# Down projection of a hybrid encoder step: two direct halves replaced by seven block products in two passes

## What is computed

```python
h = rmsnorm(x, norm_ffn_g)
gt, ffn_buf_new = causal_dwconv(h @ w_gate, ffn_buf, ffn_conv_w)
x = x + (jax.nn.silu(gt) * (h @ w_up)) @ w_down      # (640, 2816) @ (2816, 1024)
```

## Time and profile before

| | us |
|---|---|
| median of 3 runs | 945.5 (945.16 to 945.92) |
| span of the profiled execution | 943.7 |
| TensorE busy (matmuls) | 931.8, 99% |
| VectorE busy | 648.3, 69% |
| ScalarE busy | 452.1, 48% |
| GpSimd busy | 170.0, 18% |
| down projection, first to last matmul | 790.6 to 940.4 |

### The profile page before, as it was taken

One profiled execution on the slowest core, in us unless ns is written; L12 is line 12 of the kernel. 1 busy time (PEld: TensorE's weight loads), 2 busy tenths in 40 slices (PEclk: granted clock), 3 DMA queues, 4 the chain that ended last, 5 costly groups with the idle time before them and its releaser, 6 DMA issues.

```text
span 943.7 us, 16891 instructions
## 1 busy us (share of the span) xinstructions
PE 931.8 (99%) x6919; PEld 841.9 (89%) x6919; DVE 648.3 (69%) x1083; ACT 452.1 (48%) x836; POOL 170.0 (18%) x198
## 2 busy tenths in 40 slices
PE   9999999999999999999999999999999999999998
PEld 7899888998889877799888999999999999888886
DVE  7627888777775565552666999999999999435321
ACT  6634454648566454554654445444444445333310
POOL 0071101103664331000002032222222220000000
...
DMA packets 73820, 103.70 MB, mean 110 GB/s; under 512 B 2576, under 2 KB 53904, under 8 KB 73360
## 3 DMA queue, kind: packets, MB, share of 16 engines
...
## 4 chain that ended last, share of the span: by engine, by line
PE 51%; DVE 3%; ACT 2%; POOL 1%; issue 1%; ACTq 0%; POOLq 0%; DVEq 0%
PE bank L1222 8%; PE bank L1220 8%; PE bank L1221 8%; PE bank L538 5%; PE bank L537 5%; PE bank L536 5%; PE bank L484 2%; PE bank L486 1%; PE bank L485 1%; PE bank L466 1%; PE bank L562 1%; PE bank L1034 1%; PE bank L564 1%; PE bank L563 1%; PE bank L1036 1%
## 5 line engine op out<-in xcount | busy, mean ns | idle before, releaser
L2168 DVE TENSOR_TENSOR wlo<-wraw,whi 128x2048 fp32r<-128x2048 f32 (+1 forms) x56 | 126.2, 2253 | 102.2 <-ACT whi L1617 93.0
L1617 ACT ACTIVATE whi<-wraw 128x2048 fp32r<-128x2048 f32 (+1 forms) x58 | 109.3, 1885 | 101.9 <-PE bank L538 72.8
L498 PE MATMUL bank<-hhi,whi 128*128 128x320 f32 x352 | 116.4, 331 | 0.6 <-issue 0.6
L500 PE MATMUL bank<-hhi,wlo 128*128 128x320 f32 x352 | 108.7, 309 | 0.0
L499 PE MATMUL bank<-hlo,whi 128*128 128x320 f32 x352 | 108.7, 309 | 0.0
L498 PEld LDWEIGHTS bank<-hhi,whi 128*128 128x128 f32 x352 | 66.2, 188 | 5.0 <-issue 3.6
L499 PEld LDWEIGHTS bank<-hlo,whi 128*128 128x128 f32 x352 | 66.2, 188 | 3.0 <-issue 2.4
L500 PEld LDWEIGHTS bank<-hhi,wlo 128*128 128x128 f32 x352 | 66.1, 188 | 0.0
L536 PE MATMUL bank<-whi,hhi 128*128 128x512 f32 x150 | 58.4, 389 | 0.0
L537 PE MATMUL bank<-wlo,hhi 128*128 128x512 f32 x150 | 58.4, 389 | 0.0
L538 PE MATMUL bank<-whi,hlo 128*128 128x512 f32 x150 | 58.3, 389 | 0.0
...
## 6 DMA issues: line engine op xcount, KB each, us to landing
wraw<-in_w_in SPq DMA_DIRECT2D x13, 1024.0 KB, 5.5
wraw<-in_w_gate SPq DMA_DIRECT2D x11, 1024.0 KB, 5.2
wraw<-in_w_up SPq DMA_DIRECT2D x11, 1024.0 KB, 5.1
wraw<-in_w_down SPq DMA_DIRECT2D x10, 1024.0 KB, 5.1
...
wraw<-in_w_mix_out SPq DMA_DIRECT2D x4, 1024.0 KB, 6.3
...
```

Source lines behind the costliest of these rows:

```text
L498: T.matmul(o, wh[:, k, cs], hhi[:, k, hs], start=(k == 0), stop=False)
L500: ins = T.matmul(o, wl[:, k, cs], hhi[:, k, hs], start=False, stop=(k == KD - 1))
L1617: V(wv(whi, i), wv(wraw, i), ACT.Copy).then_inc(s["w_hi_ready"], 1)
L2168: V.tensor_tensor(wv(wlo, i), wv(wraw, i), wv(whi, i).bitcast(F32), ALU.subtract)\
```

## The change

The prompt's 512 rows, the 2816 numbers of the hidden width and the 1024 output columns are each split in halves. Four products of halves by halves become seven products with sums of quarters, over 11 steps each (HF = 11), since tile i of the left half goes with tile i + 11 of the right half. One product is two tiles of rows by 512 columns, six matmuls a step. The 128 sample rows are multiplied directly (`samples`, 12 matmuls a step). A weight block `B_DN[d]` now holds two row tiles (i and i + 11) over all 1024 columns, and the blocks are loaded twice: d = 0 to 10 for the first pass (products p1, p3, p5 and the samples, names `cs`), d = 11 to 21 for the second (p6, p7, p4, p2). The last two steps of the second pass are taken product by product, so that the banks end one after the other.

GpSimd makes the sums: in the first pass four of 256 numbers per partition over the activations (`first_sums`) and one of 512 over the weights (`t1_sum`); in the second pass three of 512 in place over the weight block (`block_sums`). A third sum of the activations is DVE's, within `parts_lo`. Raw blocks have four buffers now (`dn_raw`), so have their high parts (`dn_hi`). The ring of banks is fully used: the eight results p1, cs, p3, p5 (two each) take all eight, and p6, p7, p4, p2 take the same ones again. Bank by bank, ACT reads out p1 and DVE cs, p3 and p5 in round d = 13 (HF + 2), after their cuts of block 13. DVE adds the sums to the rows in rounds 14 to 17 (`more_rows`) and the rest at the end (`last_rows`).

In the diff `B_DN` is the list of the weight blocks, `s[...]` the semaphores; memory offsets, the body of `last_rows` and parts of loops that leave are cut out.

```diff
+        HF = FT // 2
+        dn_raw_at = [R2 + BLK * 4 * n for n in range(3)] + [EARLY]
+        dn_hi_at = [R2 + BLK * 4 * 3, RF, R2 + BLK * 4 * 4, R1 + 4 * BLK * 4]
...
+        def part_slot(m):
+            return 0 if m == 0 else 1 + (m - 1) % 5
+        def t1_slot(d):
+            return 0 if d == 0 else 2 - d % 2
...
+        def part_free(eng, m):
+            if m == 0:
+                passed(eng, gu_block("gate", FT // 2 - 1))
+            elif m == 1:
+                filled(eng, (("up", FT // 2 - 1), "p5"))
+            elif m < 6:
+                passed(eng, gu_block("up", FT // 2 - 1))
+            else:
+                passed(eng, B_DN[m - 5])
...
-        B_DN = [[rows(A["w_down"], k, min(4, FT - k), 512 * h) for k in range(0, FT, 4)] for h in range(2)]
...
+            blocks.append((A["w_down"].rearrange("(a f p) c -> f p a c", a=2, p=P)[n % HF], 2, D_MODEL))
+            B_DN.append(len(blocks) - 1)
...
-            down("dn", 0, B_DN[0], left_a, NT, ready_a)
-            down("dn", 1, B_DN[1], left_a, NT, ready_a)
+            def product(name, i, stationary, moving, ts=(0, 1), first=0, last=HF - 1):
+                for t in ts:
+                    c = slice(stationary[2] + t * P, stationary[2] + t * P + P)
+                    hi, lo = stationary[0][:, c], stationary[1][:, c]
+                    if i == first:
+                        take((name, t))
+                    o = bank[use[name, t][0]][:, :]
+                    T.matmul(o, hi, moving[0], start=(i == first), stop=False)
+                    T.matmul(o, hi, moving[1], start=False, stop=False)
+                    ins = T.matmul(o, lo, moving[0], start=False, stop=(i == last))
...
+            def samples(i):
...
+                    for a in range(2):
+                        ss = slice(768 + a * P, 768 + a * P + P)
+                        wh, wl = dn_weights(i, a, c)
+                        T.matmul(o, hi[:, ss], wh, start=(i == 0 and a == 0), stop=False)
+                        T.matmul(o, hi[:, ss], wl, start=False, stop=False)
+                        ins = T.matmul(o, lo[:, ss], wh, start=False, stop=(i == HF - 1 and a == 1))
...
+            for i in range(HF):
+                pe.wait_ge(s["parts_lo"], i + 1)
+                lo_cut(pe, B_DN[i])
+                product("p1", i, dn_parts(i, 0), dn_weights(i, 0, 0))
+                samples(i)
+                product("p3", i, dn_parts(i, 512), dn_weights(i, 1, 1))
+                pe.wait_ge(s["t1_lo"], i + 1)
+                ins = product("p5", i, dn_parts(i, 256), (t1_hi[t1_slot(i)][:, :], t1_lo[t1_slot(i)][:, :]))
...
+            SECOND = (("p6", 0, 0, 0), ("p7", 256, 0, 1), ("p4", 768, 1, 1), ("p2", 512, 1, 0))
+            for i in range(HF - 2):
+                d = HF + i
+                pe.wait_ge(s["parts_lo"], d + 1)
+                lo_cut(pe, B_DN[d])
...
+                step(ins, B_DN[d])
+            for name, p0, a, c in SECOND:
+                for t in range(2):
+                    for i in (HF - 2, HF - 1):
+                        d = HF + i
+                        if name == "p6" and t == 0:
+                            pe.wait_ge(s["parts_lo"], d + 1)
+                            lo_cut(pe, B_DN[d])
+                        product(name, i, dn_parts(d, p0), dn_weights(d, a, c), ts=(t,))
...
+                d = i - B_DN[0]
+                if d >= 0:
+                    if d == 3:
+                        filled(sp, (("up", FT // 2 - 1), "p5"))
+                    else:
+                        passed(sp, i - 3 if d < 3 else i - 4)
+                    D(wv(wraw, i), blocks[i][0]).then_inc(dn_loaded[d % 4], 16)
+                    return
...
+            for d in range(2, 2 * HF):
+                if d == 4:
+                    passed(sp, B_DN[0])
+                    passed(sp, gu_block("up", FT // 2 - 1))
                     sp.wait_ge(s["rows_kept"], 16)
                     D(xres[:, :, :], kept).then_inc(s["rows_back"], 16)
...
+                load_w(B_DN[d])
...
+            def first_sums(i):
+                raw, left, right = part_raw[part_slot(i)], act[:, i, 0:512], act[:, HF + i, 0:512]
+                part_free(pool, i)
+                act_made(pool, i)
+                G.tensor_tensor(raw[:, 256:512], left[:, 256:512], right[:, 256:512], ALU.add)
+                link(G.tensor_tensor(raw[:, 512:768], left[:, 0:256], right[:, 0:256], ALU.add))
+                G.tensor_tensor(left[:, 256:512], left[:, 0:256], left[:, 256:512], ALU.subtract)
+                G.tensor_tensor(raw[:, 512:768], raw[:, 512:768], raw[:, 256:512], ALU.subtract).then_inc(s["part_sums"], 1)
+            def t1_sum(d):
+                w = wv(wraw, B_DN[d])
+                dn_ready(pool, d)
...
+                else:
+                    passed(pool, B_DN[d - 2])
+                G.tensor_tensor(t1_raw[t1_slot(d)][:, :], w[:, 0, 512:D_MODEL], w[:, 0, 0:512], ALU.subtract)\
+                    .then_inc(s["t1_made"], 1)
+            def block_sums(d):
+                w = wv(wraw, B_DN[d])
+                b11, b12, b21, b22 = w[:, 0, 0:512], w[:, 0, 512:D_MODEL], w[:, 1, 0:512], w[:, 1, 512:D_MODEL]
+                dn_ready(pool, d)
+                link(G.tensor_tensor(b12, b22, b12, ALU.subtract))
+                link(G.tensor_tensor(b11, b12, b11, ALU.add))
+                G.tensor_tensor(b22, b11, b21, ALU.subtract).then_inc(s["block_sums"], 1)
+            for i in range(HF):
+                first_sums(i)
+                t1_sum(i)
+            for d in range(HF, 2 * HF):
+                block_sums(d)
...
+                d = i - B_DN[0]
+                if d >= 0:
+                    if d < HF:
+                        dn_ready(e, d)
+                    else:
+                        e.wait_ge(s["block_sums"], d - HF + 1)
...
+                    else:
+                        passed(e, B_DN[d - 4])
+                    V(wv(whi, i), wv(wraw, i), ACT.Copy).then_inc(s["w_hi_ready"], 1)
...
-                V(act_slots(n)[0], act[:, k, :], ACT.Copy).then_inc(s["ahi_ready"], 1)
+            def cut_parts(m):
...
+                if m >= HF:
+                    part_free(e, m)
+                    e.wait_ge(s["parts_lo"], i + 1)
+                    V(hi[:, :].rearrange("p (a t) -> p a t", a=2), two_halves(act, i)[:, :, 0:512], ACT.Copy)\
+                        .then_inc(s["parts_hi"], 1)
+                    return
+                e.wait_ge(s["part_sums"], m + 1)
+                V(hi[:, 0:256], act[:, i, 0:256], ACT.Copy)
+                V(hi[:, 768:D_MODEL].rearrange("p (a t) -> p a t", a=2), two_halves(act, i)[:, :, 512:TOK], ACT.Copy)
+                V(hi[:, 256:768], raw[:, 256:768], ACT.Copy).then_inc(s["parts_hi"], 1)
+            def cut_t1(d):
+                e.wait_ge(s["t1_made"], d + 1)
+                V(t1_hi[t1_slot(d)][:, :], t1_raw[t1_slot(d)][:, :], ACT.Copy).then_inc(s["t1_hi"], 1)
...
-            cut_hi(B_DN[0][1])
...
+            for d in range(1, 2 * HF):
+                cut_hi(B_DN[d])
+                cut_parts(d)
+                if d < HF:
+                    cut_t1(d)
+                if d == HF + 2:
+                    for t in range(2):
+                        b = filled(e, ("p1", t))
+                        V(sum_p1[:, t, :], bank[b][:, :], ACT.Copy).then_inc(bank_free[b], 1)
...
+                if B_DN[0] <= i < B_DN[HF]:
+                    dve.wait_ge(s["t1_made"], i - B_DN[0] + 1)
...
+            def parts_lo(m):
+                n, i = part_slot(m), m % HF
+                hi, raw, lo = part_hi[n], part_raw[n], part_lo[n]
+                dve.wait_ge(s["parts_hi"], m + 1)
...
+                V.tensor_tensor(lo[:, 0:256], act[:, i, 0:256], hi[:, 0:256].bitcast(F32), ALU.subtract)
+                V.tensor_tensor(act[:, i, 0:256], raw[:, 256:512], act[:, i, 0:256], ALU.subtract).then_inc(s["third_sums"], 1)
+                V.tensor_tensor(lo[:, 768:D_MODEL].rearrange("p (a t) -> p a t", a=2), two_halves(act, i)[:, :, 512:TOK],
+                                hi[:, 768:D_MODEL].bitcast(F32).rearrange("p (a t) -> p a t", a=2), ALU.subtract)
+                dve.wait_ge(s["third_sums"], m + 1)
+                V.tensor_tensor(lo[:, 256:768], raw[:, 256:768], hi[:, 256:768].bitcast(F32), ALU.subtract)\
+                    .then_inc(s["parts_lo"], 1)
...
-            cut_lo(B_DN[0][1])
-            nxt = B_DN[0][0] + 2
-            for n in range(LEAD, 2 * FT):
-                if n == FT + 6:
-                    dve.wait_ge(s["rows_back"], 16)
-                    for t in range(NT):
-                        add_res("dn", 0, t)
-                act_lo(n)
...
-            for i in range(nxt, NB):
-                cut_lo(i)
-            for n in range(NT):
-                add_res("dn", 1, n)
+            def to_rows(name, t, n, c, op=ALU.add):
...
+            def first_rows():
+                dve.wait_ge(s["rows_back"], 16)
+                for c in range(2):
```

(17 more changed lines are left out.)

171 lines of the change are left out of this document (112 added, 59 removed).

## The result

The changed kernel takes 974.2 us (median of 4, 972.3 to 975.9) against 945.3 us for the kernel before on the same chip: 1.030 times as long, interval 1.029 to 1.032. The profiled execution has a span of 970.5 us and is the shortest of the four (972.3 us). TensorE executes 6853 matmuls where the earlier trace rows has 6919: the 66 are gone. Its span has grown by 26.8 us all the same (943.7 to 970.5).

The account below looks back on a forecast made before the run. The prediction took the port shared by DVE and GpSimd, not PE, to set the pace: -15.0 us for fewer matmuls plus six waiting terms gave +24.8, 968.5 us on the span and 970.3 us median, range 955 to 986 us.

Parts of the forecast that it names:

- 66 matmuls less: TensorE in the down projection: 594 matmuls instead of 660, at 0.2267 us each, a gain of 15.0 us.
- start, to step 2: Start of the stage: GpSimd instructions put in between DVE's delay the parts of step 1; 5.8 us, bounds 0 and 7.4.
- steps 3 to 9: First pass: the port needs 7.6 us a step against PE's 6.8, seven times; 5.7 us, bounds 0 and 16.
- step 10: End of first pass: GpSimd's sums of blocks 11 and 12 fall between DVE's six; 11.0 against 6.8, 4.2 us.
- change of pass: Between passes: PE waits for ACT's read-out of p1, then for DVE to free the samples' bank; 8.5 us, bounds 7.2 and 12.
- steps 16 to 19: Second pass: four steps at about 7.8 us at the port against PE's 5.44; 9.7 us.
- end: Last two steps: block 21 is wanted 0.7 us after step 19 and its chain comes late; 5.9 us.
- The port: DVE's two-SBUF-input instructions and GpSimd's run one at a time, 0.14 us overlapped per change, setting the pace in both passes.
- dearer changes: Rival for the port: changes of user save 0.05 us instead of 0.14; +38 us, 984 us; 15%.
- rival 1: No exclusion in this stage: only change of pass (7.2) and end (3.4) cost; -4.4, 941.1 us, faster; 6%.
- rival 5: TensorE's clock falls in the new gaps; gaps of 5 us had no price, left within the range's upper side.
- Rival 2: Port fed without gaps: waits at start and change of pass used to run ahead; +14.6, 960 us; 22%.

Follow-up runs that it names:

- memset: Changed kernel with GpSimd's sums replaced by memsets of about the same undisturbed length, output not the reference's; 944.1 us, 0.9984 of before.
- fillers2: Changed kernel with idle matmuls put into open banks ahead of steps 10, 16, 17, 18 and 21, counts meant not to outlast PE's waits; 973.9 us.
- dve_sums: Changed kernel with all weight sums of the stage on DVE instead of GpSimd, written one block ahead of the cuts; 960.5 us.
- early: Changed kernel with ACT's read-out of p1 moved behind its cut of block 11 and DVE's first_rows ahead of its cut of block 12; 971.6 us.
- block_dve: Changed kernel with only the second pass's block_sums on DVE, first_sums and t1_sum staying on GpSimd; 968.4 us.
- end: Changed kernel with the last two steps run in three groups (p6 and p7, then p4, then p2) instead of product by product; 971.4 us.
- double_loads: Changed kernel with each block from 4 on also copied to spare memory ahead of its load, doubling the traffic; 979.9 us.

## Why the prediction was right

It said 970.3 us, slower; it is 974.2, within the range. The mechanism is shown, by memset above all. That the sum comes so close is in part luck: it is all waits at the full clock, and what was measured is 26 us of waits and about 12 us of slow matmuls. By terms, from the step starts of the profiled execution (a step's length less 6.80 or 5.44; the wait ahead of a step lies in the length of the step before it):

| term | predicted | measured |
|---|---|---|
| 66 matmuls less | -15.0 | -15.0 (66 less) |
| start, to step 2 | +5.8 | +5.4 (stage 1.3 late, steps 0 and 1 another 4.1) |
| steps 3 to 9 | +5.7 | +6.4 (7.68 us a step) |
| step 10 | +4.2 | +4.1 (10.94 us for step 9 to 10) |
| change of pass | +8.5 | +9.5 (11.81 and 9.91 us) |
| steps 16 to 19 | +9.7 | +10.0 |
| end | +5.9 | +6.4 |
| sum | +24.8 | +26.9 |

*The port.* Turns, and 0.14 us overlapped a change, are as taken. Cuts near 2.8 us were forecast and are 2.77, sums of 512 "near 2 or more" are 1.52 to 2.24 by line, two of the four lines above 2. Both rivals of its price, no exclusion (941) and dearer changes (984), are off; memset's 944 is what rival 1 would have looked like, 3 above its own sum, with waits of 9.1 us instead of 10.6 and 23 slow matmuls (4.6 us) that the sum didn't have.

*The start* was put down to step 1 alone. In truth PE stood 2.2 us already ahead of the stage's first matmul, which is 1.3 us later than in the earlier trace rows, then 2.1 ahead of step 1. Step 0 also has 1.8 us of slow matmuls. The term's size is right, its place was half wrong.

*The end* is 4.2 us of waits (0.87 and 3.36) and 1.7 of slow matmuls, where 5.9 of waits were forecast. There the port was priced too high and the clock at nothing, and the size is luck.

*The change of pass* has the two waits and the two releasers that were named, ACT L2330 and DVE L3029, but of 1.8 us each, not 5 and 3.5 (with the clock held up in step 10, as in fillers2, the first is 4.7). Most of the other 5.8 us is 14 slow matmuls in step 10 and 13 in step 11 (27 x 0.2 = 5.4). **This is the step that failed:** rival 5 had no price and stood "within the range's upper side", with the argument that the 1.08 us wait of the earlier trace rows left the clock alone. What the runs showed in its place is seven stretches at clock 0.50, about 12 us, behind waits of 1.83 us and more. In this kernel the error stayed small, because a slower PE waits less for the port. In dve_sums, where the port has slack, the slow matmuls make 7.6 us, half of what that kernel lost.

*The rest of the distance.* Of the 3.9 us between 970.3 and 974.2, 2.0 lie in the profiled execution's span (970.5 against the sum's 968.5). The other 1.95 are that the profiled execution is the fastest of four (972.3). The profiles show two places where executions of the same program differ. Step 1 takes 6.98 us there, and 8.5 to 9.6 in the profiles of early, block_dve, end, fillers2 and double_loads, which are the same up to that point, with 8 to 13 slow matmuls in it. Steps 10 and 11 take 21.7 us there and 24.5 in end: the change of pass can cost 12.3 instead of 9.5, since a turn of the port falls the other way (last point below). That these two make the spread of 972.3 to 975.9 is argued, for the other three executions have no profile.

*Rival 2*, the port fed without gaps (960): the start and the change of pass were not used to run ahead. In the stage GpSimd stood 12.1 us for PE ahead of its weight sums of the first pass (L1736) and 16.4 for the loads of blocks ahead of L1744, the buffers that the prediction held against this rival. *Gaps on transfers:* PE has none in the passes (double_loads).
